# Gate grids of a PEER layer as two products of rounded halves, the second half's one-hot rows made on GpSimd

## What is computed

```
expert = i1[ic // 16] * 128 + i2[ic % 16]
gate = softmax(vc)
a = einsum('td,thkd->thk', t, u_tab[expert])
w = gate * gelu(a)
y = einsum('thk,thkd->td', w, v_tab[expert])
```

## Time and profile before

| | before |
|---|---|
| median of 3 runs | 2213.9 us (2213.44 to 2215.03) |
| the profiled execution | 2213.12 us, its span 2211.3 us |
| PE busy | 2118.7 us, 96% of the span |
| DVE, ACT, POOL busy | 1543.2, 1234.4, 440.1 us |
| mean granted TensorE clock | 0.988 of full |

### The profile page before, as it was taken

The page is one execution under the profiler, slowest core; times in us unless marked ns, Lnnn a source line. Parts: engine busy times, 40 slices in busy tenths (PEclk is TensorE's granted clock), DMA queues, the critical chain, the costliest instruction groups (busy, mean ns, idle before and its releaser), DMA issues.

```text
span 2211.3 us, 39875 instructions
## 1 busy us (share of the span) xinstructions
PE 2118.7 (96%) x13716; PEld 1934.7 (87%) x13716; DVE 1543.2 (70%) x3008; ACT 1234.4 (56%) x2348; POOL 440.1 (20%) x184
## 2 busy tenths in 40 slices
PE   5799899999999999999999999999999999999997
PEld 4688789999999998888878978999999998888886
DVE  7688548991778877777768944899177886555554
ACT  8623544554888864444443344455488886545543
POOL 0000046988100000000000005698810000000000
PEclk9899999999999999999999999999999999999999
DMA  7723244555444467777763324455544445666563
GB/s 263 285 81 129 84 139 136 173 169 188 151 137 135 147 201 268 262 261 264 261 213 109 124 68 140 136 171 170 182 153 133 144 142 170 191 194 193 191 193 101
DMA packets 103476, 378.81 MB, mean 171 GB/s; under 512 B 11488, under 2 KB 11872, under 8 KB 102880
## 3 DMA queue, kind: packets, MB, share of 16 engines
q1 hardware_dynamic: 102672, 373.74, 51.2%
q10 hardware_dynamic: 720, 4.00, 0.5%
HBM read 375.46 MB, written 2.23 MB: 171 GB/s over the span
## 4 chain that ended last, share of the span: by engine, by line
PE 74%; issue 9%; POOL 8%; DVE 4%; ACT 2%; DMA 2%; POOLq 0%; ACTq 0%; SPq 0%; DVEq 0%
PE bank L1760 32%; PE bank L1669 8%; PE bank L1670 8%; PE bank L1671 8%; POOL split_lo L478 7%; PE bank L1733 5%; PE bank L1406 4%; DMA ring<-stream 2%; PE bank L1418 1%; PE bank L1657 1%; PE bank L1368 1%; ACT diag L536 1%; PE bank L1431 1%; PE bank L1442 1%; PE bank L1379 1%
## 5 line engine op out<-in xcount | busy, mean ns | idle before, releaser
L1669 PE MATMUL bank<-h_hi,split_hi 128*128 128x256 f32 x2304 | 666.5, 289 | 23.3 <-POOL split_lo L478 11.1
L1671 PE MATMUL bank<-h_hi,split_lo 128*128 128x256 f32 x2304 | 652.1, 283 | 0.0
L1670 PE MATMUL bank<-h_lo,split_hi 128*128 128x256 f32 x2304 | 652.0, 283 | 0.0
L1669 PEld LDWEIGHTS bank<-h_hi,split_hi 128*128 128x128 f32 x2304 | 441.8, 192 | 30.0 <-POOL split_lo L478 16.8
L478 POOL TENSOR_TENSOR split_lo<-ring,split_hi 128x1024 fp32r<-128x1024 f32 x168 | 433.3, 2603 | 172.9 <-ACT split_hi L686 172.7
L1266 DVE TENSOR_TENSOR split_lo<-ring,split_hi 128x1024 fp32r<-128x1024 f32 x248 | 303.8, 1225 | 222.0 <-ACT w_hi L784 222.0
L783 ACT ACTIVATE split_hi<-ring 128x1024 fp32r<-128x1024 f32 x248 | 263.2, 1061 | 343.0 <-PE bank L1760 339.3
L1670 PEld LDWEIGHTS bank<-h_lo,split_hi 128*128 128x128 f32 x2304 | 442.3, 192 | 0.0
L1671 PEld LDWEIGHTS bank<-h_hi,split_lo 128*128 128x128 f32 x2304 | 441.6, 192 | 0.0
L686 ACT ACTIVATE split_hi<-ring 128x1024 fp32r<-128x1024 f32 x296 | 298.7, 1051 | 196.8 <-PE bank L1671 196.7
L1760 PE MATMUL bank<-split_hi,w_hi 128*128 128x512 f32 x1024 | 315.9, 390 | 0.0
(11 more groups left out here) (271 smaller groups left out, 2526.7 us busy)
## 6 DMA issues: line engine op xcount, KB each, us to landing
ring<-stream SPq DMA_DIRECT2D x658, 512.0 KB, 3.5
ada_ring<-stream SPq DMA_DIRECT2D x48, 512.0 KB, 4.3
spill<-tables ACTq DMA_DIRECT2D x1, 1152.0 KB, 4.3
tables<-spill ACTq DMA_DIRECT2D x1, 1152.0 KB, 6.8
xT<-x_in SPq DMA_DIRECT2D x1, 1024.0 KB, 9.5
s5raw<-s5w ACTq DMA_DIRECT2D x2, 512.0 KB, 5.6
y_out<-hT SPq DMA_DIRECT2D x1, 1024.0 KB, 3.9
KM<-mixc SPq DMA_DIRECT2D x1, 576.0 KB, 7.7
```

The lines of the kernel that those rows point to most:

```text
L1669: mm(dst, hi, x_hi, start=start, stop=False, skip_group_check=not group)
L1670: mm(dst, hi, x_lo, start=False, stop=False, skip_group_check=not group)
L1671: return mm(dst, lo, x_hi, start=False, stop=stop, skip_group_check=not group)
```

## The change

The gates are split in two halves, `gate_hi` (fp32r) and `gate_lo` (the difference). DVE's `row_hots` scales with the first half. POOL makes, for the same quads, four more one-hot tiles scaled with the second (`hot_lo`); there are only four tiles of them, one for each token of a quad, so it makes those of quad q only when PE has signalled `g_ready` for quad q-1. PE makes each token's grid as two fp32r products into the same PSUM place. All hot tiles become fp32r. `pick` is copied with two rows instead of three; DVE takes the gates from PSUM itself, with four small instructions a layer.

```diff
-        hots = at_byte("hots", 72 * KB, [2, 2, 4, P])
+        hots = at_byte("hots", 72 * KB, [2, 2, 4, P], F32R)
...
+        gate_lo = [V[:, rel0:rel0 + P], S[:, 0, sk0:sk0 + P]]
+        hot_lo_cd = at_byte("hot_lo_cd", 216 * KB + 4 * (N_CONST + 38), [2, P], F32R)
+        hot_lo = [hot_lo_ab[:, 0, :], hot_lo_ab[:, 1, :], hot_lo_cd[:, 0, :], hot_lo_cd[:, 1, :]]
...
                 with pool.Fori(0, POOL_LOWS // SPLIT, 1) as i:
                     for j in range(SPLIT):
                         low(i, j)
+
+                pool.wait_ge(pick_ready, TT * (l + 1))
+                pool.wait_ge(gates_split, 2 * TT * (l + 1))
+                for q in range(QUADS):
+                    if l or q:
+                        pool.wait_ge(g_ready, QUADS * l + q)
+                    for t in range(4):
+                        at = 4 * q + t
+                        last = gp.tensor_scalar(hot_lo[t], iota, pick[:, 0, at:at + 1], gate_lo[at // P][:, at % P:at % P + 1], ALU.is_equal, ALU.mult)
+                    last.then_inc(lo_hot_ready, 1)
...
-                dve.wait_ge(pick_ready, TT * (l + 1))
+                for i in range(TT):
+                    dve.wait_ge(pick_ready, TT * l + i + 1)
+                    part = slice(i * P, i * P + P)
+                    v.tensor_copy(gate_hi[:, part], bank[:, 6 + i, 2 * P:3 * P]).then_inc(gates_split, 1)
+                    dve.wait_ge(gates_split, 2 * (TT * l + i) + 1)
+                    v.tensor_tensor(gate_lo[i], bank[:, 6 + i, 2 * P:3 * P], gate_hi[:, part].bitcast(F32), ALU.subtract)\
+                        .then_inc(gates_split, 1)
...
-                        last = v.tensor_scalar(hotA[q % 2][:, t, :], iota, pick[:, 0, at:at + 1], pick[:, 2, at:at + 1], ALU.is_equal, ALU.mult)
+                        last = v.tensor_scalar(hotA[q % 2][:, t, :], iota, pick[:, 0, at:at + 1],
+                                               gate_hi[:, at:at + 1].bitcast(F32), ALU.is_equal, ALU.mult)
...
+                    pe.wait_ge(lo_hot_ready, i * 8 + (q0 + q + 1))
                     for t in range(4):
-                        last = mm(bank[:, 4 + q % 4, t * P:t * P + P], hotB[q % 2][:, t, :], hotA[q % 2][:, t, :], start=True, stop=True)
+                        dst = bank[:, 4 + q % 4, t * P:t * P + P]
+                        mm(dst, hotB[q % 2][:, t, :], hotA[q % 2][:, t, :], start=True, stop=False)
+                        last = mm(dst, hotB[q % 2][:, t, :], hot_lo[t], start=False, stop=True)
```

More of the change, by code:

```diff
@@ L197, in build @@
         h_lo = at_byte("h_lo", 56 * KB, [KT, T], F32R)
-        hots = at_byte("hots", 72 * KB, [2, 2, 4, P])
+        hots = at_byte("hots", 72 * KB, [2, 2, 4, P], F32R)
         ada_ring = at_byte("ada_ring", 56 * KB, [2, BLOCK])
-        pick = at_byte("pick", 64 * KB, [3, T])
+        pick = at_byte("pick", 64 * KB, [2, T])
+        gate_hi = at_byte("gate_hi", 66 * KB, [T], F32R)
         res = at_byte("res", 67 * KB, [TT, 3, P])
@@ L314, in build @@
         wk = at_byte("wk", 71 * KB, [256])
+        hot_lo_ab = at_byte("hot_lo_ab", 71 * KB, [2, P], F32R)
         vals = at_byte("vals", 72 * KB, [PH, 2, PK])
@@ L343, in small_of @@
             return S[:, l, SMALL_AT[name][0]:SMALL_AT[name][1]]
+        rel0, sk0 = VEC_AT["rel"][0], SMALL_AT["sk2"][0]
+        gate_lo = [V[:, rel0:rel0 + P], S[:, 0, sk0:sk0 + P]]
+        hot_lo_cd = at_byte("hot_lo_cd", 216 * KB + 4 * (N_CONST + 38), [2, P], F32R)
+        hot_lo = [hot_lo_ab[:, 0, :], hot_lo_ab[:, 1, :], hot_lo_cd[:, 0, :], hot_lo_cd[:, 1, :]]
         ident, ones, iota = const("ident"), const("ones"), const("iota")
@@ L384, in build @@
         hot_step, column_ready = sem("hot_step"), sem("column_ready")
+        gates_split, lo_hot_ready = sem("gates_split"), sem("lo_hot_ready")
         x_done, y_copied, y_turned = sem("x_done"), sem("y_copied"), sem("y_turned")
@@ L734, in column_hots @@
                     act.wait_ge(hot_step, QUADS * l + q + 1)
-                    nc.scalar.activation(hotB[q % 2][:, :, :], hotB[q % 2][:, :, :], ACT.Relu, scale=-1.0, bias=1.0)\
+                    nc.scalar.activation(hotB[q % 2][:, :, :], hotB[q % 2][:, :, :].bitcast(F32), ACT.Relu, scale=-1.0, bias=1.0)\
                         .then_inc(column_ready, 1)
@@ L741, in _ @@
                         for i in range(TT):
-                            nc.scalar.activation(pick[:, :, i * P:i * P + P], bank[:, 6 + i, 0:3 * P].rearrange("p (r t) -> p r t", r=3),
+                            nc.scalar.activation(pick[:, :, i * P:i * P + P], bank[:, 6 + i, 0:2 * P].rearrange("p (r t) -> p r t", r=2),
                                                  ACT.Copy).then_inc(pick_ready, 1)
@@ L1203, in _ @@
                     dve.wait_ge(picked, TT * l + i + 1)
-                dve.wait_ge(pick_ready, TT * (l + 1))
+                for i in range(TT):
[5 more added lines that the diff above has]
+                        .then_inc(gates_split, 1)
+                dve.wait_ge(gates_split, 2 * TT * (l + 1))
                 pair0 = KEYS // 2 * l + FIRST_LATE // 2
```

## The result

| | before | after |
|---|---|---|
| median, us | 2214.5 (2213.4 to 2216.2) | 2490.5 (2488.8 to 2497.1) |
| ratio | | 1.1251, 95% interval 1.1229 to 1.1273 |
| late stage of a layer (first grids to the output product), us | 241.1 and 241.1 | 368.2 and 371.8 |
| PE's wait ahead of that stage, us | 0 and 0 | 9.6 and 9.5 |

A forecast was written before the change was run, and what follows sets the result against it. PE was taken to bound the late stage. The profiled 2213.1 us plus 16.8 (start), 3.4 (clock at the start) and 74 (POOL and DVE taking turns) gave 2307.5, forecast as 2308; range 2230 to 2390.

The forecast's parts named there:

- What bounds the kernel, and what is to be saved: Late stage: PE sets the end, POOL looks free; the grids, 114 us in all, are the most to save.
- PE's records at no gain: PE's grids: eight records before and after, 0.107 to 0.12 us each, set by the weight load; taken as 0.
- cheap weight loads: Rival, PE's grids: fp32r weights load at half price, -45 us; 2189 without contention (0.07), about 2263 with it (0.03).
- dear narrow products: Rival, PE's grids: fp32r products of 128 columns cost twice 0.111 us, +114 us, 2373 in all; chance 0.10.
- The start: Start of each layer's late stage: PE waits for POOL's earlier low parts, then four tiles; +16.8 us in both layers.
- 6.4 + 4c + 0.2: PE's wait at a stage's start: 6.4 us for POOL's low parts, four POOL instructions of c, 0.2 for two handovers.
- the 3.4 us for the clock: Start of each late stage: after idling, PE runs 3.5 us near half clock, half of it lost; +3.4 us in all.
- c = 0.45: Time in us of one new POOL instruction making a low one-hot tile, put below the middle of 0.30 to 0.77.
- the ceiling: Upper estimate of c, 0.77 us, from POOL's one-column instruction plus 127 columns at the two-input row's slope.
- They take turns: Every second window: POOL's tiles and DVE's two late low parts alternate, PE waits 1.19 us, 62 times; +74 us.
- POOL is slow: Rival, POOL's tiles: c from 0.65 up, 2350 to 2422 us in all; chance 0.12.

The follow-up runs named there:

- the kernel with one product: The kernel before with fp32r hot tiles and nothing else, one product a grid, the gates' second halves dropped: 2158.7 us, ratio 0.9746.
- the kernel with the start alone: The changed kernel, but POOL makes low one-hot tiles only for a layer's first quad and PE reuses them: 2239.1 us, ratio 1.0105.
- The probes: The kernel before with 72 unread POOL instructions of several forms and widths added behind the last layer's late stage: 2214.7 us beside 2214.9.
- the kernel with two tiles: The changed kernel, but POOL makes two of a quad's four low tiles after the first quad: 2302.0 us, ratio 1.0400.
- the kernel with POOL beside: The changed kernel, but PE neither waits for nor reads POOL's tiles; added waits of POOL and DVE keep the writes' order: 2298.1 us, ratio 1.0372.
- the one with the tiles handed over singly: The changed kernel, but each of the four low tiles is handed over by itself between POOL and PE: 2303.8 us, ratio 1.0405.

## Why the prediction was wrong

**What bounds the kernel, and what is to be saved:** right. POOL looked free by its busy share, and by that share it was; it isn't the share that decides but 3.09 us in a window of 2.67.

**PE's records at no gain:** right. They stay 0.11 us apart, the stage beside working POOL is 241.5, and the kernel with one product shows 0.11 for each that is dropped. The rivals that rested on cheap weight loads and on dear narrow products both fell.

**The start:** right in kind. 6.4 + 4c + 0.2 gives 9.7 with the measured c, and 9.6 was measured; the 3.4 us for the clock are near the 4.5 that the kernel with the start alone shows (23.6 - 19.1). The four new instructions of DVE cost nothing that shows there.

**c = 0.45: the step that failed.** The new instruction takes 0.773, the ceiling that I had worked out from the one-column row and the slope of the two-input row. I moved off the ceiling for two reasons that no row showed, one input instead of two and cheap operations. The probes turn both round. The forecast's formulas with c = 0.773 give 2.48 us for a window with low parts (measured 2.5) and 0.52 for one without (measured 0.74, in the 21 windows where the clock was full).

**They take turns:** right in size, wrong in its picture. POOL's tile and a low part don't alternate. DVE runs both low parts without a gap, and the one tile that begins beside the first stands behind both. The price at the mean is the forecast's 2.36 us less the overlap, as the kernel with two tiles shows with 0.98 against 0.94; that it fits so well is partly luck, since the waits run from 0.73 to 1.23 along the stage and the forecast had them all alike.

**The clock in the steady state: left out, the second step that failed.** With c at the ceiling my sum ended at 2422. The missing 68 us lie here. I had charged the clock at the start, from the earlier trace rows, and not asked whether a wait in every second quad does the same. By the trace of after the 24 matmuls of a block, summed over a layer, take 210 and 212 us instead of 181, and the grids 56 and 57 instead of 50: 35 and 38, or some 72 us of half clock. Of these my sum already had the 3.4 of the start. The slow blocks take back some 16 of the 32 us of short waits in it, since POOL is ready behind a slow block. Some 16 us are left, of which the trace shows tenths at each restart of PE and which I have not taken apart.

**The rival "POOL is slow", 2350 to 2422,** had the cause right and 0.12 of the chance. The range ended inside it, at 2390, and even its upper end was short by the clock. Its lower end was a slip as well: by the forecast's own formulas c = 0.65 gives 2361 and not 2350.

## What to carry over

An operation that an engine has never run in the trace is to be priced at the ceiling of its nearest rows until a row says otherwise, and work put on an idle engine is to be held against the window between "buffer free" and "wanted", not against its idle share. A wait that recurs costs twice, by itself and by the clock behind it: if the sum has a wait of 2 us in every turn, the work behind it has to be priced at half the clock as well (here behind two such waits of three), and handing over in smaller pieces is worth more than its own overlap. Ask too what precision the change defends; the kernel that drops it was the only one that gained.

## What the runs showed of the hardware

- On POOL a compare with a product, with one tensor as input and two pointers, costs 0.37 us and 3.3 ns a column; the product alone 0.60 us for 128 columns; a two-input subtraction 0.46.
- Between DVE's two-input low parts and POOL's one-input tiles the order of the starts decides, but the prices differ. Undisturbed a low part takes 1.21 to 1.23 us and a tile 0.79. In the 62 windows of the kernel with two tiles, a tile that began 0.18 us ahead took 0.79 and cost the low part 0.12 us. One that began 0.59 us behind the low part's start took 2.5 to 3.0. In the kernel with POOL beside, tiles that began 0.13 us or more ahead of a low part were not held up, and those 0.09 or less ahead were; the low part lost 0.17 us with the tile 0.13 ahead and nothing with it 0.29 or more ahead. So a DVE that runs two low parts back to back loses 0.17 us at most, and POOL up to 2.5 (3289 ns in that kernel). A waiting tile stood behind both low parts in the changed kernel and in the one with two tiles, and got in between them in the one with the tiles handed over singly (1.83 us, 62 times) and in some windows of the one with POOL beside; why is open.
- Four of DVE's one-hot rows take 1.24 us beside POOL's tiles and 1.11 without, where in the trace of before single rows of that kind took 2.4 beside POOL's two-input instruction.
- The Trainium skill (SBUF — State Buffer, Who interferes with whom) has it that issue order decides who blocks, and that a DVE instruction with two inputs contends with any of POOL's that reads. On DVE and POOL the second half agrees with POOL's loss. The first agrees with both tiles of the kernel with two tiles, 0.79 us for the one that was first and 2.72 for the one that was not; it doesn't tell how DVE's second low part, begun 0.67 us behind the waiting tile's start, went ahead of it.
- Waits of 2.2 to 2.8 us, once a pair, brought the granted clock of the stage to 0.88 and 0.87, with a fall behind 42 of 62; waits of 1.2 to 1.7 us brought it to 0.94, and waits of 0.66 in every quad or 0.98 once a pair left it at 0.99. In the stretch shown the fall came 1.4 us after PE had restarted; in other pairs it came during the grids.
